# Softmax normalisation of the mix stage moved from VectorE to ScalarE

## What is computed

```python
    scores = jnp.einsum('bcqhgd,bckhd->bchgqk', qc, kb,
                        preferred_element_type=jnp.float32) * (HEAD_DIM ** -0.5)
    probs = jax.nn.softmax(jnp.concatenate([scores, sink], axis=-1), axis=-1)[..., :WINDOW]
    out = jnp.einsum('bchgqk,bckhd->bcqhgd', probs.astype(v.dtype), vb)
    mix = jnp.concatenate([attn, conv], axis=-1) @ w_o[l]
    h = layer_norm(ALPHA * h + mix, ln1_g[l], ln1_b[l])
```

## Time and profile before

| | us |
|---|---|
| median of 3 timed runs | 2213.53 |
| lowest and highest of them | 2210.54, 2217.36 |
| the profiled execution | 2204.62 |
| its span in the trace | 2202.8 |
| of it TensorE busy | 2019.2 (92%) |
| of it VectorE busy | 1277.4 (58%) |
| of it ScalarE busy | 732.9 (33%) |
| of it GpSimd busy | 662.5 (30%) |

### The profile page before, as it was taken

How to read it: one execution, slowest core, us unless ns; L and a number is a source line. 1 busy time by engine, 2 the same in 40 slices (tenths; PEclk the granted TensorE clock), 3 DMA queues, 4 the chain that set the end, 5 groups by cost and what they waited for, 6 DMA issues and landing times. The chain is left out here.

```text
span 2202.8 us, 25782 instructions
## 1 busy us (share of the span) xinstructions
PE 2019.2 (92%) x9240; PEld 1657.5 (75%) x9240; DVE 1277.4 (58%) x1343; ACT 732.9 (33%) x1071; POOL 662.5 (30%) x410
## 2 busy tenths in 40 slices
PE   4899996498988589999999999999999699999998
PEld 3788885476766478888888888888888578788886
DVE  8699874689999535343433334343434454556686
ACT  4555553354444342121112111211121233323354
POOL 5597774234444300110210110102101166530000
PEclk9999998699999889999999999999999899999999
DMA  6401112533333251211221111112111354477653
GB/s 236 151 15 62 67 67 82 143 103 95 124 120 93 93 186 46 98 67 38 82 90 38 67 74 69 67 38 105 67 38 69 124 164 142 137 223 246 188 183 138
DMA packets 187214, 233.15 MB, mean 106 GB/s; under 512 B 10976, under 2 KB 130144, under 8 KB 186592
## 3 DMA queue, kind: packets, MB, share of 16 engines
q1 hardware_dynamic: 161216, 196.71, 27.2%
q10 hardware_dynamic: 25952, 35.86, 4.5%
HBM read 147.98 MB, written 84.54 MB: 106 GB/s over the span
## 5 line engine op out<-in xcount | busy, mean ns | idle before, releaser
L1502 PE MATMUL u_mm<-u_hT_hi,u_w_hi 128*128 128x512 f32 x1408 | 549.1, 390 | 15.4 <-DVE u_hT_lo L1459 15.4
L1502 PE MATMUL u_mm<-u_hT_lo,u_w_hi 128*128 128x512 f32 x1408 | 548.9, 390 | 0.0
L1502 PE MATMUL u_mm<-u_hT_hi,u_w_lo 128*128 128x512 f32 x1408 | 548.7, 390 | 0.0
L1425 DVE TENSOR_SCALAR u_y<-u_z,u_taps,u_bias 128x2048 f32<-128x2048 f32 x43 | 57.9, 1346 | 529.9 <-ACT u_z L1373 529.9
L1373 ACT COPY u_z<-u_mm 128x512 f32<-128x512 f32 x176 | 103.4, 588 | 741.2 <-PE u_mm L1502 741.2
L1502 PEld LDWEIGHTS u_mm<-u_hT_hi,u_w_hi 128*128 128x128 f32 x1408 | 264.9, 188 | 70.8 <-DVE u_hT_lo L1459 15.8
L1502 PEld LDWEIGHTS u_mm<-u_hT_lo,u_w_hi 128*128 128x128 f32 x1408 | 265.0, 188 | 55.2
L1502 PEld LDWEIGHTS u_mm<-u_hT_hi,u_w_lo 128*128 128x128 f32 x1408 | 265.0, 188 | 55.1
L1863 PE MATMUL d_y<-d_wd_hi,d_a_hi 128*128 128x512 f32 x616 | 242.6, 394 | 26.9 <-DVE d_a_lo L1745 26.8
L1863 PE MATMUL d_y<-d_wd_hi,d_a_lo 128*128 128x512 f32 x616 | 241.9, 393 | 0.0
L1863 PE MATMUL d_y<-d_wd_lo,d_a_hi 128*128 128x512 f32 x616 | 241.8, 393 | 0.0
(11 more groups left out here) (193 smaller groups left out, 2872.0 us busy)
## 6 DMA issues: line engine op xcount, KB each, us to landing
d_a_raw<-gated_scr SPq DMA_DIRECT2D x56, 704.0 KB, 5.0
u_w_raw<-w_up SPq DMA_DIRECT2D x44, 512.0 KB, 4.5
d_wd_raw<-w_down SPq DMA_DIRECT2D x88, 256.0 KB, 5.1
gated_scr<-u_s SPq DMA_DIRECT2D x41, 512.0 KB, 2.7
gated_scr<-u_y SPq DMA_DIRECT2D x20, 512.0 KB, 3.4
a_xs<-x SPq DMA_DIRECT2D x16, 512.0 KB, 4.4
m_h_in<-h_scr SPq DMA_DIRECT2D x16, 512.0 KB, 3.5
h_scr<-m_r ACTq DMA_DIRECT2D x16, 512.0 KB, 3.6
```

Of the source, the lines that this page charges most:

```text
L1425: nc.vector.tensor_scalar(y[:, m, :], z[:, m, PAD:], tap(s, PAD), bias[:, bass.ds(s, 1)], ALU.mult, ALU.add).then_inc(conv_seq, 1)
L1502: last = nc.tensor.matmul(mm[m][n][:], w[:, m, k, :], h[:, k, bass.ts(n, BLK)], start=(k == 0 and w is w_hi and h is hT_hi), stop=(k == KT ...
```

## The change

The in-place multiplication of `prob` by `inv` leaves VectorE and goes to ScalarE. VectorE did it in one instruction for each group, 128 partitions by 512 columns, with `inv` spread along the keys. ScalarE takes it in four instructions for each group, 128 columns each, where the instruction's scale operand is the one number per partition of that head. VectorE's reciprocal now signals a new semaphore `inv_ok`, for which ScalarE waits; `prob_ok`, for which TensorE's transposes wait, is raised by the last of the four. On ScalarE both groups stand after the second exponential and ahead of the copies of `probT`.

```diff
@@ ScalarE
+            def probs(n, g):
+                act.wait_ge(inv_ok, NKV * n.t + (g + 1))
+                for a in range(GROUPS):
+                    v = prob[:, g, a, 0:KEYS]
+                    last = nc.scalar.activation(v, v, ACT.Copy, scale=inv[:, g, a:a + 1])
+                last.then_inc(prob_ok, 1)
+
...
                 exps(n, 0)
                 conv_root(n)
                 exps(n, 1)
+                for g in range(NKV):
+                    probs(n, g)
                 probs_T(n)
                 attn_hi(n)
@@ VectorE
             def soft_at(n, g, k):
-                return n.t * (NKV * 5) + (3 * g + k)
+                return n.t * (NKV * 4) + (3 * g + k)
...
                 nc.vector.tensor_reduce(den[:, g, :], prob[:, g, :, :], AX.X, ALU.add).then_inc(soft_seq, 1)
-                dve.wait_ge(soft_seq, n.t * (NKV * 5) + (3 * NKV + 2 * g + 1))
-                nc.vector.reciprocal(inv[:, g, :], den[:, g, :]).then_inc(soft_seq, 1)
-                dve.wait_ge(soft_seq, n.t * (NKV * 5) + (3 * NKV + 2 * g + 2))
-                nc.vector.tensor_tensor(prob[:, g, :, 0:KEYS], prob[:, g, :, 0:KEYS], along(inv[:, g, :], KEYS), ALU.mult).then_inc(prob_ok, 1)
+                dve.wait_ge(soft_seq, n.t * (NKV * 4) + (3 * NKV + g + 1))
+                nc.vector.reciprocal(inv[:, g, :], den[:, g, :]).then_inc(inv_ok, 1)
```

More of the change, by code:

```diff
@@ L684, in phase_mix @@
         conv_hi_ok, conv_lo_ok, attn_hi_ok, attn_lo_ok = (sem("m_" + n) for n in ("conv_hi", "conv_lo", "attn_hi", "attn_lo"))
-        vw_ok, shift_ok, exp_ok, prob_ok, probT_ok = (sem("m_" + n) for n in ("vw", "shift", "exp", "prob", "probT"))
+        vw_ok, shift_ok, exp_ok, inv_ok, prob_ok, probT_ok = (sem("m_" + n) for n in ("vw", "shift", "exp", "inv", "prob", "probT"))
         resid_ok, lv_ok, ly_ok, norm_ok, scaled_ok, h1_ok, h1T_ok = (sem("m_" + n) for n in ("resid", "lv", "ly", "norm", "scaled", "h1", "h1T"))
```

## The result

| | before | changed |
|---|---|---|
| median of the timed runs, us | 2213.81 (4 runs) | 2180.72 (4 runs) |
| lowest and highest | 2210.54, 2217.36 | 2179.21, 2182.04 |
| the profiled execution | 2204.62 | 2182.04 |
| busy in the mix stage (390 to 764 and 390 to 740 us), VectorE / ScalarE, us | 320 / 166 | 298 / 207 |

The kernel before has its three timed runs and one more. The ratio is 0.985 (95% interval 0.9833 to 0.9867). The two profiled executions lie 22.6 us apart. These two differences are the subject of the rest: the forecast of the path was close, the forecast of the median was not.

The account below looks back on a forecast made before the run. Bound: in the mix stage TensorE's second transposes wait for VectorE's multiplication, held by GpSimd. Tiles 2 to 14 give 18.2, tile 15 2.0, tile 0 -0.3: 19.9, so 20 us; 2213.5 - 20 = 2193.5 us, range 2182 to 2206.

Parts of the forecast that it names:

- What holds the ring: Mix stage's loop per tile (scores, softmax, transposes, values, output projection): TensorE waits 14 times, 2.1 us each, for VectorE's multiplication.
- The turns with GpSimd: VectorE instructions with two SBUF inputs run only between GpSimd instructions; the multiplication takes 1.86 and 1.91 us, not 0.69.
- ScalarE's cost: Eight scaled copies of 128 columns per tile, 394 ns each, starting 0.297 us apart: 2.47 us; bounds include 3.84 us above.
- What is late next: VectorE's conv_norm moves under GpSimd's row and waits its turns, 4.86 us instead of 2.33, cutting 2.1 us gained to 1.4.
- Rival 1: VectorE isn't held again in conv_norm, TensorE is last: gain 29 to 33 us, 2180 to 2184; chance 0.15.
- The gain of a tile: Tiles 2 to 14 of the mix stage: 1.4 us each, 13 x 1.4 = 18.2 us.
- The last step: Tile 15, with no L787 behind L803, so L115 doesn't wait: the whole 2.1 us count, entered as 2.0.
- The entrance: Tile 0, where VectorE's multiplication takes only 0.69 us: the second group ready 0.3 us later; tile 1 nothing.
- the sum: Gains over the mix stage's tiles: 18.2 + 2.0 - 0.3 = 19.9, so 20 us.
- the last of the sum: 20 us taken from the timed runs' median instead of the profiled execution: 2213.5 - 20 = 2193.5 us.
- offset: The profiled execution, 2204.6 us, was 8.9 us under the timed runs' median; the forecast was made for the median.

## Why the prediction was wrong, step by step

- **What holds the ring** (the wait for L1024 in 14 tiles): right. It is gone, and no other wait of its size has come up for the transposes.
- **The turns with GpSimd**, read from the 0.55 us behind each GpSimd instruction: right, shown by the reciprocals in PSUM (0.69 us in place of 1.87).
- **ScalarE's cost**: 2.47 us forecast for eight, 2.47 measured, 391 ns each where 394 were worked out from the earlier trace rows.
- **What is late next**: forecast 0.5, 2.4 and 1.6 us for L111, L113 and L115, measured 0.50, 2.42 and 1.53. From `conv_norm`'s first instruction to the start of its last it takes 4.86 us, the number forecast; the new wait for `attn_lo` is there; L803 at 2.38 us. Rival 1 didn't come about. The time landed on its number, which is a coincidence and no support for its mechanism: L113 and L115 were held, and L803 began 0.11 us ahead of L113 (612.98 and 613.09), the order and the margin forecast.
- **The gain of a tile**: forecast 1.4 us. The tiles of before without a fall of the clock take 20.66 us on average, those of the changed kernel 19.25: 1.42. 13 x 1.42 = 18.4. The last step from L801 to L801 went from 21.20 to 19.08, 2.1 us (forecast 2.0). The entrance lost 0.2 (58.61 us from the first weight load for the scores to the first L801, 58.78 after; forecast 0.3). That is 20.3 us where the sum had 19.9. Two falls at 1.4 us in the first trace of before make it 23.1, and the profiled executions differ by 22.6; the rest is small differences in the other stages.
- **The step that failed is the last of the sum**, "the forecast is made for the median: 2213.5 - 20". It carried the 8.9 us between the profiled execution and the median over to the changed kernel as an offset that no edit touches, and it gave TensorE's clock no term. But the kernel before loses time at its median to falls of TensorE's clock, which come behind the very wait that the sum had just taken away. Two of them, 2.8 us, were in the profiled execution already, and the changed kernel's median has no offset over its profile: it lies 1.3 us below. The 22.04 us tile and the 0.91 of granted clock in two of the stretches were in the trace of before, and the spread of 7 us in three runs was in its times; neither was priced. Filling the wait shows 8.5 us for this at the median. By an estimate from these numbers 8.5 - 2.8 = 5.7 of the 8.9 us of offset were such falls. The term was put at 0 and measures 8.5.

With it the median's sum is 20 + 8.5 = 28.5 of 31.2 to 33.1 us. The remaining 3 to 5 us aren't accounted for; the part behind the mix stage differs by up to 6 us between traces (1442.8 to 1448.6), which is enough to hide them, but nothing here assigns them.

## What to carry to other kernels

A VectorE instruction with two inputs in SBUF that lasts nearly three times its usual length and ends a fixed time after a GpSimd instruction is probably waiting for its turn, as here; putting one of its two inputs into PSUM ended that in three kernels of this study, and may be worth as much as moving it to another engine. When an instruction leaves a row, look at what then slides under the other engine's work: here a chain of small dependent instructions took back a third of the gain, and the edit that freed them was worth nothing visible until then. When a kernel's times spread and its profile lies at the edge of them, ask which of its waits the spread comes from before adding the offset to a forecast.

## What the runs showed of the hardware that wasn't expected

- TensorE's clock fell from 2.4 to 1.2 GHz behind waits of 2.1 us, in 2 to 5 of 14 tiles of an execution, for about 3.5 us, at 1.4 us of tile time each. Behind two waits of about 0.5 and 1.7 us it still fell in 2 of 13 tiles of the one trace; with the wait cut to 0.54 us by filling it fell in none.
- Useless work made a kernel faster: 26 us more of matmuls, 8.5 us less of time.
- In `conv_norm`'s chain of dependent VectorE instructions one after the other lost a turn, short as they are: 128 columns, 0.29 us of work, took 2.42 us behind a GpSimd instruction of 2.38, and the next took 1.53 behind one of 1.60.

The fastest kernels of the study are the changed one with the refinement's tiles in PSUM, 2171.7 us, and the kernel before with these and the reciprocals in PSUM, 2171.0 us, both about 1.85% under the kernel before.
